# Token mixer of a two-layer diffusion backbone on one core: norms beside the products, gates and projections inside the attention steps

## The chip, the cores and the metric

The kernel runs on one core of a Trainium2 chip. Its time is the device time of one execution in microseconds (us). A core has TensorE (PE in the profile, its weight loads PEld), VectorE (DVE), ScalarE (ACT), GpSimd (POOL) and SyncE (SP, here the queue that loads weights). Each engine works through its own instructions in order and waits on semaphores that other engines raise.

## The reference, cut to what matters

Two layers over 640 tokens of width 1024: 512 latent tokens (tiles t = 0 to 3) and 128 context tokens (tile 4, called NS), in float32. The names on the left are those used below.

```python
mod = silu(cond) @ w_mod + b_mod                  # 6 x 1024 for each of 2 conditionings
sh1, sc1, g1, sh2, sc2, g2 = split(mod, 6)
h = rmsnorm(x, norm1_g) * (1 + sc1) + sh1
aq, ak, av, bu, bv, cq, ck, cv, gl = split(h @ w_in)     # 1792 columns (QKV), then 3 x 1024 (gates)
aq, ak, cq, ck = rmsnorm of each head of 64, then rotary angles
oa = windowed attention(aq, ak, av, cache_a, sink)       # branch A: 6 heads, blocks t-1, t, t+1, cache
ob = gelu(bu) * (w_s @ rmsnorm(gelu(bv)) + b_s)          # branch B
oc = full attention(cq, ck, cv, cache_c)                 # branch C: 6 heads, 4 blocks and cache
merged = sigmoid(gl[0])*(oa @ w_a_o) + sigmoid(gl[1])*(ob @ w_b_o) + sigmoid(gl[2])*(oc @ w_c_o)
x = x + g1 * (merged @ w_out)
h2 = rmsnorm(x, norm2_g) * (1 + sc2) + sh2
x = x + g2 * expert_choice_moe(h2)                       # 16 experts, 80 rows each, 96 weight chunks of 2 MB
```

## The kernel before

Both layers run the same program. Its stages follow each other on TensorE. Weights come in chunks of 8 x 128 rows by 512 columns (2 MB) into a ring of three slots, in one fixed order, issued by SP when a chunk's slot is free.

- **Conditioning, first part.** `mod_group` (line 617) multiplies `condT` (2 columns for each of 8 row blocks) by a 512-column chunk: 8 float32 products, each of which the trace shows as two instructions, 16 in all. Only 2 of the array's 128 columns are used. Four groups (MOD1) give shift and scale of the first norm; DVE adds the bias (L1205, L1209), 16 small transposes (L650) turn them into columns, and `h_out`/ACT L959 apply them to the transposed tiles (L605).
- **Products in three parts.** `group` (L628) multiplies one token tile by 256 columns: 24 instructions, high x high, high x low, low x high, in the rounded format. ACT makes the high part of the weights (WH, L947), DVE the low part (WL, L1183), both in two buffers of their own, so a ring slot is free as soon as it is split. QKV takes 7 x 5 = 35 groups; two PSUM banks of 256 columns are emptied in turn by ACT (L977) and DVE (L1233).
- **The rest of the conditioning and the norms.** Eight more `mod_group`s (MOD2), three of them right behind QKV, four between the turned heads and one inside attention; ACT copies the rows (L995), POOL adds biases (L494). After all of QKV, ACT does gelu and squares (L982, L989), DVE the sums (L1241), POOL the gains (L474), and DVE rotates queries and keys of both branches (L1254 to L1268, 5 tiles x 2 branches); TensorE turns them (L605).
- **Attention.** 60 units, one head of one tile each (`ORDER`). `scores` (L698, two heads side by side in the array's two row halves), masks (L706, float32), `reduce_max` (L1287) and the negative maximum (L1289, L1291) on DVE, exp on ACT (L1024), `turn` (L715), its copy out on DVE or ACT in turn (L1300, L1038), `weigh` (L726), and the scaled output (L1316). Nothing else but `mlp` (L686, branch B) and turned outputs lies among these steps.
- **Gates and projections.** 60 gate groups (L628, `split` again) and 60 projections (L775: float32, 2 or 3 row blocks of w_o by 256 columns, that is 4 or 6 instructions), ACT's tanh (L1061) and DVE's product (L1341, L1344), in the order A, B, C; group o+1 is issued ahead of projection o.
- **Output, router, experts.** 20 groups with w_out, second norm, router, top-k, then the experts (L857), with their own splits (L1090, L1440).

Of the kernel before, what the change touches and what calls it, by code (L numbers as in the profile page):

```python
# [5 lines left out]
D = 1024  # L20
# [8 lines left out]
MOD2_FIRST = 3  # L29
MOD2_AT = {2 * i + 1: MOD2_FIRST + i for i in range(MOD2 - MOD2_FIRST - 1)}  # L30
# [13 lines left out]
C_QKV = MOD1  # L44
C_MOD2 = C_QKV + (QU + 1) // 2
C_GATE = C_MOD2 + MOD2
C_WO = C_GATE + 9
C_MOE = C_WO + 2
CHUNKS = C_MOE + E * FFC
assert CHUNKS % RING == 0 and FFC % RING == 0 and C_MOE % RING == 0  # L50
LOADS = CHUNKS // RING
BRANCH = ((0, 1, 2), (6, 7), (3, 4, 5))


# [5 lines left out]
def unit_chunk(u):  # L60

    if u < U_GATE:
        return C_QKV + u // 2, u % 2
    if u < U_WO:
        b, q = divmod(u - U_GATE, 4)
        return C_GATE + 3 * b + 2 * (q // 2), q % 2
    return C_WO + (u - U_WO) // 2, (u - U_WO) % 2

G_QKV = MOD1
G_MOD2 = G_QKV + QU * NT
G_GATE = G_MOD2 + MOD2
G_WO = G_GATE + GU * NT
GROUPS = G_WO + WU * NT
GB = ((GROUPS + 1) // 2, GROUPS // 2)


def in_bank(g, b):

    return (g + 1 - b) // 2


def wo_group(w, t):

    return G_WO + (w * NT + t if w < 2 else 2 * NT + 2 * t + w - 2)


def last_group(u):

    if u < U_GATE:
        return G_QKV + u * NT + NT - 1
    if u < U_WO:
        return G_GATE + (u - U_GATE) * NT + NT - 1
    return wo_group(u - U_WO, NT - 1)

T_MOD, T_WS, T_CK, T_QK = 0, 1, 2, 3
T_MLP = T_QK + 2 * NT  # L100
T_O = T_MLP + NT
TQ = T_O + 2 * NT
# [4 lines left out]
UNITS = NT * 12  # L107
# [4 lines left out]
PAIR_ROWS = [6 * br + 3 * kv + g for br in range(2) for g in range(3) for kv in range(2)]  # L112
ORDER = [u for i in range(6) for u in [(i // 2, PAIR_ROWS[6 * (i % 2) + j]) for j in range(6)] +
         [(NS, PAIR_ROWS[2 * i + j]) for j in range(2)]] + [(NS - 1, r) for r in PAIR_ROWS]
LAST = [max(i for i, u in enumerate(ORDER) if u[0] == t) for t in range(NT)]

TURNS = {LAST[t] + 5 + 3 * h + 5 * (t == NS): (t, h) for t in (0, 1, 2, NS) for h in range(2)}
TURN_NO = {u: i for i, u in enumerate(list(TURNS.values()) + [(NS - 1, 0), (NS - 1, 1)])}
MLP_AT = {4 * t + 2: t for t in range(NT)}


def sinks_until(u):

    return sum(r < 6 for _, r in ORDER[:u + 1])


def unit(u):

    t, r = ORDER[u]
    br, h = divmod(r, 6)  # L130
    kv, g = divmod(h, 3)
# [6 lines left out]
    return t, br, kv, g, blocks  # L138


def build(nc, A, outs, scratch):
# [9 lines left out]
    with ctx:  # L151
# [7 lines left out]
        f32r = mybir.dt.float32r  # L159
        ring = sb("ring", [128, RING, KB, 512])  # L160
# [8 lines left out]
        qpair = EP[:, 512:1280].rearrange("p (b n) -> p b n", b=2)  # L169
        tmp = EP[:, 0:512]  # L170
        sqa, sqc, sqv = EP[:, 0:512], EP[:, 512:1024], EP[:, 1280:1536]
        hm = EP[:, 0:2 * D].rearrange("p (b n) -> p b n", b=2)
        gate_s = EP[:, 0:512].rearrange("p (b n) -> p b n", b=2)
        gated = EP[:, 512:768]
# [20 lines left out]
        condT = sb("condT", [128, 2 * KB])  # L195
# [13 lines left out]
        mx = sb("mx", [128, 4])  # L209
        nm = sb("nm", [128, 4])  # L210
        sm = sb("sm", [128, 4])
        es = sb("es", [128, 4])
        den = sb("den", [128, 1])
        rden = sb("rden", [128, 4])

        with ExitStack() as first:
            def sa(name, shape, dt=f32, scope=first):
                return scope.enter_context(nc.sbuf_tensor(name, shape, dt))

            with ExitStack() as rounded:  # L220
                HTH = sa("HTH", [128, NT, KB, 128], f32r, rounded)
            HT = sa("HT", [128, NT, KB, 128])
            with ExitStack() as split:
                WH = sa("WH", [128, 2, KB, 256], f32r, split)
                WL = sa("WL", [128, 2, KB, 256], f32r, split)
            MB = sa("MB", [128, 8 * D])
            Y = sa("Y", [128, NT * QKV])
            QK = sa("QK", [128, 8 * 640 + 2 * 768])
# [12 lines left out]

        modrow = Y[0:2, 0:2 * D]
        nrow1 = Y[0:2, 2 * D:3 * D]
        modrow2 = MB[0:2, 0:4 * D]
        bmod2 = MB[0:2, 4 * D:8 * D]
        nrow2 = bmod2[:, 0:D]
        gain2_part = bmod2[:, D:2 * D]
        y = Y[:, :].rearrange("p (t c) -> p t c", t=NT)
        merged = Y[:, 0:NT * D].rearrange("p (t d) -> p t d", t=NT)
        x1 = merged  # L250
        g1bc = Y[:, NT * D:(NT + 2) * D].rearrange("p (s d) -> p s d", s=2)
# [11 lines left out]

        ring_ready = [sem(f"ring_ready{s}") for s in range(RING)]
# [7 lines left out]
        par2_ready = sem("par2_ready")  # L272
# [6 lines left out]
        kv_saved = sem("kv_saved")  # L279
# [4 lines left out]
        cond_ready = sem("cond_ready")  # L284
        g_done = sem("g_done")
        g_free = [sem(f"g_free{b}") for b in range(2)]
        tq_done = sem("tq_done")
        tq_free = sem("tq_free")
# [5 lines left out]
        ROOTS = 2 * NT + 1  # L294
# [7 lines left out]
        gs_ready = sem("gs_ready")  # L302
# [8 lines left out]
        s_done = sem("s_done")  # L311
        nm_ready = sem("nm_ready")
# [6 lines left out]
        opj_done = sem("opj_done")  # L319
        opj_free = sem("opj_free")  # L320
# [32 lines left out]
        def chunk_src(l, c, e=None):  # L353

            if e is not None:
                w = (A["w_gate"], A["w_up"], A["w_gate"], A["w_up"], A["w_down"], A["w_down"])[c]
                n = (0, 0, 1, 1, 0, 1)[c]
                return w[l, e].rearrange("(k p) n -> p k n", p=128)[:, :, 512 * n:512 * n + 512]
            k0, k1 = 0, KB
            if c < C_QKV:  # L360
                w, lo, n = A["w_mod"], 512 * c, 512
            elif c < C_MOD2:
                w, lo = A["w_in"], 512 * (c - C_QKV)
                n = min(512, QKV - lo)
            elif c < C_GATE:
                w, lo, n = A["w_mod"], 512 * (c - C_MOD2 + MOD1), 512
            elif c < C_WO:
                br, i = divmod(c - C_GATE, 3)
                if i == 1:
                    w, lo, n, k0, k1 = A["w_o"], 0, D, BRANCH[br][0], BRANCH[br][-1] + 1  # L370
                else:
                    w, lo, n = A["w_in"], QKV + D * br + 256 * i, 512
            else:
                w, lo, n = A["w_out"], 512 * (c - C_WO), 512
            return w[l].rearrange("(k p) n -> p k n", p=128)[:, k0:k1, lo:lo + n]

        def slot_as(c, k, n):

            return ring[:, c % RING].rearrange("p k n -> p (k n)")[:, 0:k * n].rearrange("p (k n) -> p k n", k=k)
# [1153 lines left out]
```

## Time and profile before

| what | value |
|---|---|
| runs | 2824.15, 2825.93, 2835.42 us, median 2825.93 |
| profiled execution, its own time | 2830.99 us |
| its span, first to last instruction | 2829.2 us |
| mean granted TensorE clock | 0.929 of 2.4 GHz |
| instructions | 37290 |

The profile shows one execution. PE busy is a matmul's time from start to modelled end; consecutive matmuls overlap, so the distance between starts (the pitch) is what one costs. PEclk is the granted clock of TensorE as a share of 2.4 GHz; 0.5 is 1.2 GHz. "x" counts instructions. A run of n instructions on one row lasts (n - 1) pitches and one duration.

### The profile page before, as it was taken

To read this page: it belongs to the slowest core of one execution; us is meant where nothing else is said; L and a number is where in the kernel's file an instruction comes from. 1 tells how busy PE (TensorE), PEld (TensorE's weight loads), DVE (VectorE), ACT (ScalarE), POOL (GpSimd) and SP (SyncE) were. 2 spreads that over 40 slices of the span, in tenths; PEclk is the share of its full clock that TensorE was granted. 3 is DMA by queue.
4 is the path that set the end of the run, shared out by engine and by line. 5 is a ranking of instruction groups with operands and counts; after the bars stand their busy time and mean duration, and the time that the engine had idled before them with its cause. 6 is when DMAs were issued, how large, how long until landed. Compare 5 with 4: busy or idle time off the path is not lost.

```text
span 2829.2 us, 37290 instructions
## 1 busy us (share of the span) xinstructions
PE 2528.3 (89%) x14671; PEld 1915.1 (68%) x14671; DVE 1669.0 (59%) x2087; ACT 1195.6 (42%) x1414; POOL 378.3 (13%) x265
## 2 busy tenths in 40 slices
PE   5998899999949999999959989899999499999996
PEld 1964778989936666666529448799898266666664
DVE  2346542223567888889731664522345788888885
ACT  2222332112236666667531223411122366666664
POOL 1034000000021122211110430000000201221111
PEclk9998879999969999999979976999998699999998
DMA  8144000221539999999852530002224499999996
GB/s 299 46 169 156 1 1 16 75 82 38 224 111 333 359 372 373 368 370 377 309 204 75 175 120 1 1 16 75 83 100 165 165 336 358 373 370 374 374 375 224
DMA packets 267985, 568.76 MB, mean 201 GB/s; under 512 B 7056, under 2 KB 9280, under 8 KB 267760
## 3 DMA queue, kind: packets, MB, share of 16 engines
q1 hardware_dynamic: 251856, 512.25, 50.3%
q0 software_dynamic: 14416, 49.12, 5.9%
q10 hardware_dynamic: 1584, 5.57, 0.6%
q8 instruction: 92, 1.51, 0.2%
q14 instruction: 37, 0.30, 0.0%
HBM read 545.36 MB, written 26.80 MB: 202 GB/s over the span
## 4 chain that ended last, share of the span: by engine, by line
PE 47%; DMA 23%; DVE 16%; issue 7%; ACT 6%; DVEq 0%; ACTq 0%; SPq 0%; POOL 0%; POOLq 0%
PE ps L628 23%; DMA ring<-in_w_down 11%; DMA ring<-in_w_up 9%; PE ps L857 6%; DVE w_lo L1440 6%; PE ps L775 5%; ACT w_hi L1090 4%; PE ps L698 3%; PE ps L617 2%; PE ps L726 2%; PE ps L715 2%; PE ps L605 1%; DVE mx L1287 1%; PE ps L706 1%; DVE EP L1260 1%
## 5 line engine op out<-in xcount | busy, mean ns | idle before, releaser
L1440 DVE TENSOR_TENSOR w_lo<-ring,w_hi 128x2048 fp32r<-128x2048 f32 x378 | 859.0, 2285 | 165.1 <-ACT w_hi L1090 162.5
L1090 ACT ACTIVATE w_hi<-ring 128x2048 fp32r<-128x2048 f32 x384 | 722.0, 1916 | 350.0 <-DMA ring<-in_w_down 169.6
L857 PE MATMUL ps<-w_hi,xT 128*80 128x512 f32 x2048 | 647.9, 395 | 5.8 <-issue 3.5
L628 PE MATMUL ps<-WH,HTH 128*128 128x256 f32 x1840 | 541.9, 295 | 3.3 <-DVE WL L1183 3.3
L628 PE MATMUL ps<-WL,HTH 128*128 128x256 f32 x1840 | 520.6, 283 | 0.0
L628 PE MATMUL ps<-WH,HTL 128*128 128x256 f32 x1840 | 518.4, 282 | 0.0
L857 PEld LDWEIGHTS ps<-w_hi,xT 128*80 128x80 f32 x2048 | 305.4, 149 | 178.7 <-issue 9.2
L857 PE MATMUL ps<-w_lo,xT 128*80 128x512 f32 x1024 | 405.1, 396 | 0.0
L857 PE MATMUL ps<-w_hi,hT 128*80 128x512 f32 x1024 | 329.6, 397 | 29.9 <-DVE hT L1446 12.6
L628 PEld LDWEIGHTS ps<-WH,HTH 128*128 128x128 f32 x1840 | 349.7, 190 | 6.8 <-DVE WL L1183 3.7
L628 PEld LDWEIGHTS ps<-WH,HTL 128*128 128x128 f32 x1840 | 353.2, 192 | 0.0
L628 PEld LDWEIGHTS ps<-WL,HTH 128*128 128x128 f32 x1840 | 349.4, 190 | 3.1
L580 POOL DMA_INDIRECT x_save<-EP,idx x32 | 125.8, 3931 | 922.4 <-DVE EP L1455 922.4
L857 PEld LDWEIGHTS ps<-w_hi,hT 128*80 128x80 f32 x1024 | 152.8, 149 | 122.9 <-DVE w_lo L1440 15.8
L617 PE MATMUL ps<-ring,condT 128*2 128x512 f32 x384 | 174.4, 612 | 40.2 <-DMA ring<-in_w_mod 21.1
L857 PEld LDWEIGHTS ps<-w_lo,xT 128*80 128x80 f32 x1024 | 152.6, 149 | 79.5 <-issue 1.6
L1061 ACT ACTIVATE EP<-ps 128x256 f32<-128x256 f32 x120 | 45.9, 384 | 377.8 <-PE ps L628 377.8
L857 PE MATMUL ps<-w_lo,hT 128*80 128x512 f32 x512 | 202.6, 396 | 0.0
L1024 ACT ACTIVATE EP<-ps,nm 128x640 f32<-128x640 f32 (+3 forms) x120 | 77.4, 645 | 237.9 <-PE ps L715 83.7
L775 PE MATMUL ps<-ring,QK 128*128 128x256 f32 x640 | 163.1, 389 | 15.7 <-DMA ring<-in_w_o 14.4
L1344 DVE SCALAR_TENSOR_TENSOR EP<-EP,ps 128x256 f32<-128x256 f32 x80 | 33.6, 421 | 218.4 <-PE ps L775 218.4
L1287 DVE TENSOR_REDUCE mx<-ps 128x1 f32<-128x640 f32 (+3 forms) x120 | 75.9, 632 | 138.9 <-PE ps L698 138.9
(173 smaller groups left out, 2618.7 us busy)
## 6 DMA issues: line engine op xcount, KB each, us to landing
ring<-in_w_gate SPq DMA_DIRECT2D x64, 2048.0 KB, 9.4
ring<-in_w_up SPq DMA_DIRECT2D x64, 2048.0 KB, 9.5
ring<-in_w_down SPq DMA_DIRECT2D x64, 2048.0 KB, 11.5
ring<-in_w_mod SPq DMA_DIRECT2D x24, 2048.0 KB, 8.1
ring<-in_w_in SPq DMA_DIRECT2D x18, 2048.0 KB, 8.3
ring<-in_w_out SPq DMA_DIRECT2D x4, 2048.0 KB, 13.8
ring<-in_w_o SPq DMA_DIRECT2D x4, 1536.0 KB, 6.9
Y<-x_save POOLq DMA_DIRECT2D x10, 512.0 KB, 3.9
```

What stands on the lines that cost most here:

```text
L580: pool.indirect_dma_start(xs_d, bass.IndirectOffsetOnAxis(ap=idx[0:CE, e:e + 1], axis=0), eo[0:CE, e % 2], None, compute_op=ALU.add).then_ ...
L617: last = nc.tensor.matmul(ps[0:2, bank], condT.rearrange("p (s k) -> p k s", s=2)[:, k], ring[:, c % RING, k], start=k == 0, stop=k == KB - 1)
L628: last = nc.tensor.matmul(ps[:, g % 2, 0:256], a[:, t, k], w[:, u % 2, k], start=k == 0 and i == 0, stop=k == KB - 1 and i == 2)
L698: last = nc.tensor.matmul(ps[:, 2 * kv + i // 4, 128 * (i % 4):128 * (i % 4) + 128], qoT[r, 3 * br + g, 128 * t:128 * t + 128], kT[r, br, ...
L715: last = nc.tensor.transpose(ps[:, 4 + i // 4, 128 * (i % 4):128 * (i % 4) + 128], prob[:, u % 2, 128 * i:128 * i + 128], ident[:, :])
L726: last = nc.tensor.matmul(ps[:, 6, 0:64], probT[:, u % 2, 128 * i:128 * i + 128], v, start=i == 0, stop=i == len(blocks) - 1)
L775: last = nc.tensor.matmul(ps[:, 4 + o % 2, 0:256], qoT[:, k, 128 * t:128 * t + 128], w[:, i, 256 * q:256 * q + 256], start=i == 0, stop=k ...
L857: last = nc.tensor.matmul(ps[0:CE, bank], lhs[:, a, kb], w[:, u, k], start=kb == 0 and i == 0, stop=kb == KB - 1 and i == 2)
L1024: nc.scalar.activation(prob[:, i % 2, 0:n], ps[:, s0:s0 + 2].rearrange("p b n -> p (b n)")[:, 0:n], ACT.Exp, bias=nm[:, m], scale=SCALE, a ...
L1090: nc.scalar.activation(w_hi[:, u % UB], ring[:, raw[0], 4 * (u % 2):4 * (u % 2) + 4], ACT.Copy).then_inc(hi_ready, 1)
L1287: link(nc.vector.reduce_max(mx[:, m], ps[:, s0:s0 + 2].rearrange("p b n -> p (b n)")[:, 0:n], AX.X))
L1440: TT(w_lo[:, u % UB], ring[:, raw[0], 4 * (u % 2):4 * (u % 2) + 4], w_hi[:, u % UB].bitcast(f32), ALU.subtract).then_inc(lo_ready, 1)
```

## The change

The arithmetic is the same. What moves:

- `mod_group` puts the 8 row blocks into four column groups of the array (`tile_position=(0, 32 * q)`, `condT` widened to 32 columns), so that partial sums stand in four groups of PSUM partitions. They are added by a product with `fold` (for MOD1 merged with the transposes, for MOD2 `fold_rows`, one float32 product of 512 columns each). MOD2's eight groups and folds now stand inside the QKV loop (`MOD_AT`, `FOLD_AT`), through one ring slot.
- Ring chunks have hand-written slots (`PRE`); low parts overwrite the chunk (`ringL` lies on `ring`), so a slot is free only when its groups are done.
- QKV's PSUM is emptied 512 columns at a time from three banks. Squares, sums, rotation and turning of branch A and the gelu lie inside the QKV loop; branch C's norms come at the start of attention, its rotation and turning in steps 1 to 6.
- Attention goes in 30 steps, one for each pair of heads, A first and then C. Each step has three gaps (`FILL`) with gate groups, projections, branch B and turned outputs: 42 gates and 40 projections; 18 gates and 20 projections follow behind (`TAIL`). The order of branches is B, A, C. There is one PSUM bank for gates (6) and one for everything else (7). The mask product is in the rounded format.

```diff
+PRE = [(("mod", 0), 0), (("mod", 1), 1), (("mod", 2), 2), (("mod", 3), 0), (("qkv", 0), 1), (("qkv", 1), 2),
+       (("mod", 4), 0), (("mod", 5), 0), (("mod", 6), 0), (("qkv", 2), 1), (("mod", 7), 0), (("mod", 8), 0),
...
+SPLIT_AT = {-(-5 * u // 2): u + 1 for u in range(U_GATE - 1)}
+SPLIT_AT[15] = U_GATE
+MOD_AT = {3 + 4 * i: i for i in range(MOD2)}
+FOLD_AT = {5 + 4 * i: i for i in range(MOD2)}
+KA_AT = {25 + 2 * t: t for t in range(NT)}
...
+put(0, 0, "gate", 0)
+put(0, 0, "gate", 1)
+put(0, 0, "gate", 2)
+for n, (j, gap) in enumerate([(j, gap) for j in (1, 2, 3) for gap in (0, 2)] + [(j, 0) for j in range(4, 15)]):
+    put(j, gap, "gate", 3 + n)
+for t in range(NT):
+    put(2 + t, 0, "kc", t)
+    put(4 + t, 1, "mlp", t)
+    put(5 + t, 1, "mix", t)
+for n, (j, gap) in enumerate([(6, 2), (7, 2), (8, 2), (9, 2)] + [(j, gap) for j in range(10, 15) for gap in range(3)] +
+                             [(15, 0)]):
+    put(j, gap, "proj", n)
...
+LAGGED = lambda s: [x for o in range(20) for x in ([("gate", 20 * s + o)] + ([("proj", 20 * s + o - 1)] if o else []))] + \
+    [("proj", 20 * s + 19)]
+for n, (kind, i) in enumerate(LAGGED(1)):
+    put(15 + (n + 1) // 3, (n + 1) % 3, kind, i)
+TAIL = LAGGED(2)
...
@@ TensorE @@
+                        q = k % 4
+                        last = nc.tensor.matmul(ps[32 * q:32 * q + 32, bank], condT[:, k], ring[:, SLOT["mod", c], k],
+                                                start=k < 4, stop=k >= 4, tile_position=(0, 32 * q))
...
+                def fold_rows(i):
+                    pe.wait_ge(part_ready, l * MOD2 + i + 1)
+                    pe.wait_ge(mrow_ready, l * MOD2 + i)
+                    nc.tensor.matmul(ps[0:2, 5], fold[:, 0:2], modpart2, start=True, stop=True).then_inc(mrow_done, 1)
...
+                def gate(o):
+                    v, t = divmod(o, NT)
+                    if l or o:
+                        pe.wait_ge(gs_ready, l * GROUPS_G + o)
+                    group(ps[:, 6, 0:256], U_GATE + v, t).then_inc(gt_done, 1)
...
+                for j in range(NP + 1):
+                    if j < NP:
+                        scores(j)
+                    for kind, i in FILL[j][0]:
+                        extra(kind, i)
+                    if j:
+                        turn(2 * j - 2)
+                    for kind, i in FILL[j][1]:
+                        extra(kind, i)
+                    if j:
+                        turn(2 * j - 1)
+                    for kind, i in FILL[j][2]:
+                        extra(kind, i)
+                    if j:
+                        weigh(j - 1)
@@ ScalarE, QKV loop @@
+                    if p % 2 == 0:
+                        act.wait_ge(g_done, l * QG + min(2 * p + 2, QG))
+                        qkv_out(nc.scalar.copy, p).then_inc(g_free[p % 3], 1)
+                        if p:
+                            mod_part(p // 2 - 1)
...
+                split(U_GATE + 1)
+                evacuated(act, l, QP - 1)
...
+                nc.scalar.activation(sqa, y[:, :, CQ:CQ + 512], ACT.Square).then_inc(sq_ready, 1)
+                root(NT + 1, rs100[:, :, 8:20], st100[:, :, 8:20])
@@ ScalarE, attention @@
+                for j in range(NP + 1):
+                    for kind, i in FILL[j][0]:
+                        extra(kind, i)
+                    if j < NP:
+                        exps(j, 0)
+                    for kind, i in FILL[j][1]:
+                        extra(kind, i)
+                    if j:
+                        turned(j - 1)
+                    if j < NP:
+                        exps(j, 1)
+                    for kind, i in FILL[j][2]:
+                        extra(kind, i)
@@ VectorE @@
+                dve.wait_ge(s_done, l * NP + j + 1)
+                    link(nc.vector.tensor_reduce(mx[:, b], s_pair[:, :, 0:n], axis=AX.X, op=ALU.max))
...
+                split(U_GATE + 1)
+                sums(2, sqa, 8, 8)
+                mean_heads(8, 20)
+                dve.wait_ge(sd_ready, l * ROOTS + NT + 2)
+                nc.vector.reciprocal(rs100[:, :, 8:20], rs100[:, :, 8:20]).then_inc(rs_ready, 1)
...
+                    if j < NP:
+                        peak(j)
+                    for kind, i in FILL[j][0]:
+                        extra(kind, i)
+                    if j:
+                        turned(j - 1)
+                    if 1 <= j <= NT:
+                        rotate(1, j - 1)
...
```

## Rows read from the trace of the kernel before

**Rows 1.** The page, part 4: the chain that ended last, by line
```profile
PE ps L628 23%; DMA ring<-in_w_down 11%; DMA ring<-in_w_up 9%; PE ps L857 6%; DVE w_lo L1440 6%; PE ps L775 5%; ACT w_hi L1090 4%; PE ps L698 3%; PE ps L617 2%; PE ps L726 2%; PE ps L715 2%; PE ps L605 1%; DVE mx L1287 1%; PE ps L706 1%; DVE EP L1260 1%
```

**Rows 2.** Stages of layer 0: window, busy us (x) by engine, PEclk, DMA share, GB/s
```profile
0.00:78.20 78.20, 41.03 (x129) 15.23 (x130) 23.66 (x49) 26.22 (x46) 10.03 (x24) 0.91 0.77 271
78.20:178.60 100.40, 100.40 (x841) 100.27 (x841) 20.89 (x24) 16.19 (x23) 0.00 (x0) 0.98 0.21 74
178.60:242.50 63.90, 55.21 (x155) 13.62 (x154) 55.16 (x77) 23.34 (x52) 40.30 (x43) 0.98 0.63 223
242.50:442.90 200.40, 175.51 (x1217) 149.25 (x1217) 100.59 (x318) 67.94 (x188) 18.23 (x13) 0.79 0.07 23
442.90:704.30 261.40, 251.32 (x1826) 240.60 (x1825) 72.31 (x122) 49.29 (x83) 3.13 (x6) 0.98 0.15 53
704.30:829.70 125.40, 80.78 (x625) 79.32 (x626) 73.69 (x142) 25.95 (x34) 24.56 (x24) 0.77 0.44 161
829.70:1411.90 582.20, 561.95 (x2552) 361.70 (x2552) 487.19 (x314) 389.83 (x284) 91.58 (x29) 0.99 1.00 353
1411.90:1481.30 69.40, 40.30 (x126) 14.74 (x126) 23.89 (x49) 24.63 (x44) 8.88 (x14) 0.76 0.63 223
```

**Rows 3.** The chain in order of time, layer 0: start, us, what
```profile
27.43 29.58 PE ps L617 x64
...
78.19 100.48 PE ps L628 x840
...
472.86 1.29 PE ps L775 x6
474.15 2.83 PE ps L628 x24
```

**Rows 4.** The same, layer 1
```profile
1444.92 15.37 PE ps L617 x32
```

**Rows 5.** TensorE's groups by shape, both layers
```profile
L726 PE MATMUL ps<-Y,EP 128*128 128x64 f32 x672 | 105.7, 299 | 7.5 <-DVE Y L1316 7.0
L698 PE MATMUL ps<-QK 64*128 64x128 f32 x864 | 94.6, 356 | 28.4 <-ACT EP L1024 26.5 <-ACT QK L1009 1.5
L715 PE MATMUL ps<-ident,EP 128*128 128x128 f32 x432 | 86.6, 328 | 13.4 <-DVE EP L1300 7.2 <-ACT EP L1038 3.9 <-ACT EP L1024 2.1
L726 PE MATMUL ps<-cacheV,EP 128*128 128x64 f32 x192 | 42.4, 307 | 0.0
```

**Rows 6.** Timeline at full clock, heads with five blocks: start, us, instruction
```profile
1801.49 0.79 ACT L1024 ACTIVATE EP<-ps,nm 128x640 f32<-128x640 f32 x1 [1.17 <-DVE nm L1291]
...
1802.27 0.69 ACT L1038 ACTIVATE EP<-ps 128x640 f32<-128x640 f32 x1
...
1802.42 1.39 PE L698 MATMUL ps<-QK 64*128 64x128 f32 x20 [0.34 <-ACT EP L1024]
...
1803.84 0.82 DVE L1287 TENSOR_REDUCE mx<-ps 128x1 f32<-128x640 f32 x1 [1.36 <-PE ps L698]
...
1805.75 0.73 PE L715 MATMUL ps<-ident,EP 128*128 128x128 f32 x5 [0.18 <-DVE EP L1300]
...
1806.32 1.00 PE L726 MATMUL ps<-Y,EP 128*128 128x64 f32 x8
...
1807.16 0.39 PE L726 MATMUL ps<-cacheV,EP 128*128 128x64 f32 x2
```

**Rows 7.** ScalarE's groups, all of the run
```profile
L1061 ACT ACTIVATE EP<-ps 128x256 f32<-128x256 f32 x120 | 45.9, 384 | 377.8 <-PE ps L628 377.8
...
L995 ACT ACTIVATE MB<-ps 2x512 f32<-2x512 f32 x16 | 9.3, 584 | 73.1 <-PE ps L617 73.1
...
L926 ACT ACT_TABLE_LOAD x6 | 7.7, 1283 | 0.1
```

**Rows 8.** VectorE's groups by shape, 160 to 460 us
```profile
L1241 DVE TENSOR_REDUCE st<-EP 128x8 f32<-128x512 f32 x10 | 6.4, 681 | 6.3 <-ACT EP L989 6.3
```

**Rows 9.** The page, part 6: loads, KB, median us from issue to landing
```profile
ring<-in_w_mod SPq DMA_DIRECT2D x24, 2048.0 KB, 8.1
```

More of the change, by code:

```diff
@@ L28 @@
 MOD1, MOD2 = 4, 8
-MOD2_FIRST = 3
-MOD2_AT = {2 * i + 1: MOD2_FIRST + i for i in range(MOD2 - MOD2_FIRST - 1)}
+MODS = MOD1 + MOD2
 QU = QKV // 256
@@ L106, with pair @@
 HQ = 6 * NT
-UNITS = NT * 12
+NP = 2 * 3 * NT
+UNITS = 2 * NP
+GROUPS_G = GU * NT
 EPS = 1e-6
 SCALE = HD ** -0.5
[L112 to L131, printed above, removed]
+def pair(j):
+    n, g = divmod(j, 3)
+    br, t = divmod(n, NT)
     if t == NS:
@@ L381, in raw_of, with evacuated @@
+        def evacuated(engine, l, p):
+            for b in range(3):
+                n = len(range(b, p + 1, 3))
+                if n:
+                    engine.wait_ge(g_free[b], l * (QP // 3) + n + 1)
         def raw_of(j, b, first, s):
@@ new lines, in turn @@
+                def turn(v):
+                    n = len(pair(v // 2)[3])
+                    pe.wait_ge(e_ready, l * UNITS + v + 1)
+                    if l or v:
+                        pe.wait_ge(pt_evac, l * UNITS + v)
+                    for i in range(n):
+                        last = nc.tensor.transpose(psf[:, 1536 + 128 * i:1536 + 128 * i + 128],
+                                                   prob[:, v % 2, 128 * i:128 * i + 128], ident[:, :])
+                    last.then_inc(pt_done, 1)
@@ new lines, in weigh @@
+                def weigh(j):
+                    t, br, g, blocks = pair(j)
+                    pe.wait_ge(pt_evac, l * UNITS + 2 * j + 2)
+                    if l or j:
+                        pe.wait_ge(o_evac, l * NP + j)
+                    if j == 0:
+                        pe.wait_ge(mrow_ready, (l + 1) * MOD2)
+                    for kv in range(2):
+                        for i, b in enumerate(blocks):
+                            c = (AV, CV)[br] + 64 * kv
+                            v = cacheV[:, br, 64 * kv:64 * kv + 64] if b == NT else y[:, b, c:c + 64]
+                            last = nc.tensor.matmul(ps[:, 5, 64 * kv:64 * kv + 64], probT[:, kv, 128 * i:128 * i + 128], v,
+                                                    start=i == 0, stop=i == len(blocks) - 1)
+                    last.then_inc(pv_done, 1)
@@ new lines, in extra @@
+                def extra(kind, i):
+                    if kind == "gate":
+                        gate(i)
+                    elif kind == "proj":
+                        project(i)
+                    elif kind == "mlp":
+                        mlp(i)
+                    elif kind == "mix":
+                        mixed(i)
+                    elif kind == "out":
+                        outputs(i)
+                    else:
+                        turn_qk(1, i)
+                for j in range(NP + 1):
[13 more added lines that the diff above has]
+                        weigh(j - 1)
@@ L790, in _ @@
+                for kind, i in TAIL:
+                    extra(kind, i)
+                    if kind == "proj" and i > GROUPS_G - NT:
+                        merged_tile(i - GROUPS_G + NT - 1)
                 merged_tile(NT - 1)
```

1096 lines of the change are left out of this document (577 added, 519 removed).

## Prediction

> **What bounds the kernel now.** I read the chain of waits by line first: the three-part products (L628) lead it with 23% [rows 1], and behind them come weight loads of the experts. Then the stages of layer 0 [rows 2]. The experts move 353 GB/s with the DMA share at 1.00 for 582.2 us; the change doesn't touch them, and layer 1 repeats all stages. What is left is about 830 us a layer, and there three stages stand in a row that could overlap. In 178.6 to 242.5 us DVE is busy for 55.2 of 63.9 us with norms and rotation, and TensorE only has conditioning groups. In attention (200.4 us) all engines wait for each other in turn, and the granted clock averages 0.79 (of the two levels, 1.2 GHz for 42% of the time). The gates and projections (261.4 us) keep TensorE fully busy while DVE and ACT are idle for three quarters. So the question is how much real TensorE work attention holds.
>
> **Prices per instruction.** A group of 24 takes 2.83 us, a projection of 6 takes 1.29 us, which is 0.215 us for 256 columns in float32 [rows 3]; branch B's of 4 instructions take 0.86. With five blocks, turning a head costs 0.57 us (from its start to that of the weighing) and weighing it 10 x 0.105 = 1.05 us (8 of them in 0.84) [rows 6]. The 20 instructions of scores for two heads end in 1.39 us, at most 0.07 each. Alone, 128 columns would cost half of 0.215, that is 0.107, so the two row halves of the array do work side by side.
>
> **Conditioning in column groups.** 64 instructions of MOD1 last 29.58 us at 0.43 us or more each, one after another [rows 3], so a group of 16 costs 6.9 us. Column groups are not in this trace. The bounds are 0.107 us an instruction (all four overlap, 1.7 us a group) and 0.43 (none does, 6.9 us). Since the scores' halves overlap nearly in full, I take a factor of about 3, 2.2 us a group.
> The Trainium skill (TensorE: Matmul & The Clock Gate, "Measured speedup vs the span model" and "Why this matters for your kernels") has 3.07 times for four row tiles and 2.38 times for three column tiles; by 3.07 a group would cost 2.2 us and the time stay as forecast, by the lower bound of the row it would be some 8 us less, by the upper bound 100 more. The same skill (TensorEngine Tiling (Array Packing), "Key Properties") says that a change of tiling mode drains the array, which speaks against eight tiled groups amid QKV; no row here prices it.
> MOD1 in layer 0: the first chunk arrives at 27.4 us. The fourth can load only when the first group is done (32 us, at the low clock the engine starts with) and lands 8.1 us later [rows 9], so the groups end near 43.5 instead of 57.0 us. The fold inside the transposes adds 56 small instructions, some 4 us (at 0.07). QKV starts near 68.4 instead of 78.2 us: **-10**. In layer 1 DVE frees the banks only after the norm's first tiles, and the last two groups start at 1444.9 whatever they cost, and take 15.4 us [rows 4]; they would take 8 at the low clock, and the fold takes 5 back: **-2**.
>
> **QKV with MOD2 and the norms inside.** 35 groups: 99 us, as now (100.4). Eight conditioning groups 8 x 2.2 = 18, eight folds of two instructions of 512 columns, 8 x 0.86 = 7, five turned tiles 2.5 us. A wait is added: fold i stands right behind group 5 + 4i, and ACT makes its operand only after it has emptied the PSUM that this same group fills, two copies of 0.58 us [rows 7] and two handoffs. So TensorE, with all of QKV queued behind it, waits some 1.5 us eight times: 12 us. The sum is 138 against 100.4 + 63.9 = 164.3 us [rows 2]: **-26**. Squares, sums and the rotation of branch A are hidden beside 138 us of products, in which DVE has only 21 us of its own [rows 2] and gets about 45 more. The one load slot for conditioning chunks is covered too: 8.1 us to land [rows 9], one needed each 14 us. POOL's stores and reloads of bias rows have 28 us for each buffer.
>
> **Attention with the gaps filled.** Its own TensorE work: 432 scores at 0.065, 216 turns at 0.114, 432 weighings at 0.105 (half of the counts of both layers [rows 5]) make 28 + 25 + 45 = 98, masks, branch B and turned tiles about 15 (some 136 instructions at 0.11): 113 us. So of the 200.4 us over 85 are waits, though PE shows busy for 175.5. Filled in: 42 gates 119 us, 20 projections of B 17, 20 of A 26. Sum **275 us**. I add where the order makes TensorE wait all the same:
> - The start. ACT's split for gate 5 waits for all of QKV, then come squares of 2560 columns (2.2 us at ACT's rate of 640 columns in 0.79 less its start), DVE's split and sums (2.8 us, four to five times the 0.68 of 512 columns [rows 8]), and the root with a table load of 1.28 us [rows 7], then another for exp. Gates 0 to 2 share one bank, and gate 1 waits for the first tanh, which is queued behind all this on ACT. Step 0 takes about 19 us where its work is 10: +9.
> - Steps with four blocks or fewer. After scores (1.2) and a gate (2.8), ACT does tanh (0.38), exp, the copy of turned probabilities and exp again (0.7, 0.6, 0.9 with its row sum), so the pair is done near 8 us, and weighing waits about 1 us for the copy. 15 such steps: +12.
> - Steps 15 to 26, five blocks: scores 1.3, turns 1.1, weighing 2.1, and three items of the gaps 6.1 us, 10.6 us in all. Beside it DVE has its maximum of 1280 columns (2 x 0.82, less a start), and ACT 2 x 0.79 + 0.69 + 1.5 x 0.38 = 2.8 us and the reads of two row sums [rows 6, 7]: both are covered, and TensorE bounds the step. Handoffs 0.5 each: +6.
> - The last three steps have one block and few items: +8.
> Together **310 us**. Behind it the tail: 18 gates and 20 projections are 51 + 26 = 77, and 3 for the last tile: **80**. The stage now takes 200.4 + 261.4 = 461.8; 310 + 80 = 390: **-72**. I take the clock as full, since in the stages of dense products it stands at 0.98 [rows 2].
>
> **Edits costed at nothing.** Low parts in place hold each slot until its groups are done; a load (8 us) is covered by the five or more groups, 14 us, that still run from the other slot, and o_w for branch A and C by steps 15 and 29 to 30. If that cover went, each would cost up to its landing time of 8 us. Output stage, router and experts (125.4 + 582.2 us) keep their order; their first chunks load later, yet within these 125 us.
>
> **The sum.** Layer 0: 10 + 26 + 72 = 108; layer 1: 2 + 26 + 72 = 100; together 208 us. The span of 2829.2 becomes 2621; its own time lies 2 us above, the median of the runs 5 below that: **2618 us**.
>
> **Rivals.**
> - *Busy is busy.* If TensorE's 175.5 busy us in attention were work and not latency, the stage would be 175.5 + 251.3 = 427 and win 35 instead of 72 us a layer: 2618 + 74 = 2692. For it: the busy share of 88%. Against it: the pitches above. Chance 0.08.
> - *The order across engines bounds the steps.* Gates have one bank, so each waits for a tanh that ACT reaches only in its queue, behind exps that wait for DVE's maximum, which waits for DVE's part of a split. If each of 31 steps lost 2 us more: 2 x 62 us, 2742. For it: this kind of wait makes up attention today. Against it: the steps' margins of 2 to 5 us. Chance 0.14.
> - *Column groups don't overlap.* Then MOD2 costs 8 x 4.7 = 38 us a layer more and MOD1 gives nothing and takes its fold, 24 in both layers: 2618 + 100 = 2718. Chance 0.07. This is also the case in which the change doesn't do what it says.
> - *Slower: the low clock.* If the mixed steps kept TensorE at 1.2 GHz for all of attention, its 275 us of work a layer would take twice as long, since 1.2 GHz is half of the upper level: +550, 3170 us. It decides once about 105 extra us a layer are lost, that is with the low level for 38% of that work; today the stage is at 42%. Against it: the gates put dense products into every gap. Chance 0.04.
>
> **Numbers.** Forecast 0.65, busy 0.08, order 0.14, column groups 0.07, low clock 0.04, no change 0.02. In the forecast's own case the waits I added (2 x 35 + 2 x 12) may vanish, and full overlap gives 8 more: 2530 at the low end; the high end of this case is 2670. The range must take in busy and most of the column case: 2530 to 2720. Times within 0.5% of 2826 can't be told from no change. Faster 0.94, same 0.02, slower 0.04.
>
> **What would show it.** Right: the stage between QKV and attention is gone, QKV lasts near 138 us with eight short idle spots before the folds, waiting for ACT's copy; L617's counterpart has a pitch near 0.14 us; steps 15 to 26 last about 11 us each with PE's instructions end to end; PEclk near 1 in attention; the first gate's tanh waits some 7 us behind the root. Wrong: steps of 13 us or more with TensorE waiting for tanh or for copies; PEclk at 0.5 in long stretches; a pitch of 0.43 in the conditioning groups; TensorE waiting for chunks whose slot is held too long.

## The result, and the profile of the kernel after

The kernel after takes 2705.54 us in the median of 4 runs (2702.21 to 2706.07), beside 2829.61 us for the kernel before on the same chip: a ratio of 0.9559 (95% interval 0.9535 to 0.9583). It is faster by 124 us; the forecast was a gain of 208 us, that is 2618 us with a range of 2530 to 2720. The profiled execution's span went from 2829.2 to 2704.3 us.

The head of the page of the kernel after, and its chain by line, beside [rows 1]:

```profile
PE 2400.3 (89%) x14743; PEld 1875.3 (69%) x14743; DVE 1604.9 (59%) x1841; ACT 1187.4 (44%) x1350; POOL 352.1 (13%) x257
...
PEclk8899899999779999999959998999996899999998
...
PE ps L708 24%; DMA ring<-in_w_up 12%; DMA ring<-in_w_down 10%; PE ps L995 6%; DVE w_lo L1675 6%; PE ps L853 5%; ACT w_hi L1265 4%; PE ps L832 4%; PE ps L796 3%; PE ps L677 2%; PE ps L692 1%; DMA ring<-in_w_mod 1%; PE ps L816 1%; PE ps L931 1%; DVE EP L1690 1%
```

L708 is the old L628 (products in three parts), L692 the old L617 (conditioning groups), L853 the old L775 (projections), L832 and L796 weighing and scores. PEclk is not near 9 throughout: the digits 7 to 5 mark stretches at the lower of the two levels, 1.2 GHz, and some lie in stages that I had costed at 2.4 GHz.

The stages of layer 0 after, in the columns of [rows 2]; the last row is the conditioning stage of layer 1:

```profile
0.00:82.00 82.00, 39.13 (x184) 26.54 (x185) 24.05 (x54) 26.20 (x46) 12.04 (x28) 0.79 0.72 259
82.00:220.10 138.10, 128.34 (x1005) 107.04 (x1003) 46.14 (x59) 31.69 (x39) 14.79 (x25) 0.99 0.44 154
220.10:562.70 342.60, 313.94 (x2422) 286.85 (x2421) 142.72 (x303) 104.13 (x244) 16.23 (x25) 0.95 0.13 44
562.70:647.20 84.50, 82.33 (x598) 78.25 (x598) 29.16 (x52) 17.66 (x31) 2.87 (x4) 1.00 0.17 61
647.20:771.20 124.00, 79.60 (x618) 78.24 (x616) 73.26 (x141) 25.42 (x34) 25.74 (x23) 0.76 0.41 151
771.20:1349.10 577.90, 559.88 (x2556) 362.17 (x2559) 486.98 (x314) 389.42 (x284) 102.42 (x29) 0.99 1.00 356
1349.10:1420.90 71.80, 34.00 (x184) 25.19 (x184) 23.54 (x50) 24.59 (x44) 10.88 (x18) 0.61 0.60 213
```

| stage of layer 0 | before | forecast | after |
|---|---|---|---|
| until QKV starts | 78.2 | 68.4 | 82.0 |
| QKV, norms, conditioning | 164.3 | 138 | 138.1 |
| attention with its fill | 200.4 + 261.4 (gates behind it) | 310 | 342.6 |
| tail of gates and projections | in the above | 80 | 84.5 |
| w_out, router | 125.4 | 125.4 | 124.0 |
| sum, until the experts | 829.7 | 721.7 | 771.2 |

So layer 0 misses 49.5 us: 13.6 ahead of QKV, 0.1 in QKV, 32.6 in attention, 4.5 in the tail, less 1.4 behind it. Layer 1 shows the same: from QKV to w_out it takes 564.0 us against 627.4 before, and its conditioning stage is 2.4 us longer than before instead of 2 us shorter. The experts are as before (577.9 and 582.2 us).

**Ahead of QKV.** The chain of the kernel after in order of time:

```profile
28.05 3.67 PE ps L692 x16
...
31.74 12.43 DMA ring<-in_w_mod
...
44.21 3.41 PE ps L692 x16
...
48.97 0.31 PE ps L737 x2
...
63.27 0.51 PE ps L737 x2
63.78 0.87 PE ps L740 x8
```

The groups are short, but the chunks of weights land only at 28.1 to 44.2 us, so the groups end at 47.6 us instead of the forecast 43.5: the fourth chunk lands 12.43 us after the first group has freed its slot, where the prediction took 8.1 [rows 9]. Then the fold inside the transposes (L735 sums the four column groups while it turns them, L737 adds the bias) takes from 48.6 to 63.8 us, 15.2 us where the prediction had 4. From the end of the groups to QKV it takes 34.4 us, forecast were 24.9. The windows of the fold tell why: 0.155 us an instruction at first (0.31 for two), 0.26 later, and between them, at 50.4 us, the granted clock falls to its lower level.

```profile
48.60:50.90 2.30, 2.30 (x16) 2.19 (x15) 0.14 (x1) 1.28 (x1) 0.00 (x0) 0.95 1.05 387
50.90:63.80 12.90, 12.90 (x52) 12.51 (x53) 2.29 (x1) 2.43 (x2) 0.00 (x0) 0.50 0.66 243
```

**Attention.** The distances between the first scores of one step and of the next, taken from the timeline of L796 (us, step 0 first): 19.3, 11.7, 10.6, 11.4, **11.9, 12.5, 16.1, 14.7, 15.5**, 9.1, 11.2, 10.0, 9.0, 9.3, 8.1, 9.6; then twelve with the work of five blocks, mean 11.2; then 6.4 and the last one. Step 0 was forecast at 19 and the twelve at 11.1. What stands out are steps 4 to 8, 70.7 us. Of these the chain in order of time shows step 6 (its first scores start at 298.04 us):

```profile
302.22 5.04 PE ps L708 x24
307.26 0.45 PE ps L677 x4
...
307.73 0.45 ACT QK L1120
...
308.94 0.40 ACT QK L1202
...
309.48 1.09 PE ps L862 x8
...
310.79 0.67 DVE Y L1526 x3
...
311.60 1.10 PE ps L853 x4
312.70 1.73 PE ps L832 x16
```

L677 (turned keys and mixed tiles), L862 (branch B's mix) and L853 (a projection) all write the one bank 7. So TensorE writes it, ACT empties it (L1120, L1202), TensorE writes it again, DVE empties it (L1526), and only then come projection and weighing. TensorE waits 1.8 us (307.71 to 309.48; 0.67 us of it is an exp that stands between ACT's two copies in its queue) and then 1.0 us (310.57 to 311.60). And the gate group L708 in front takes 5.04 us where it takes 2.83 at 2.4 GHz: the granted clock is at 1.2 GHz from 296.2 to 306.4 us and again from 323.5 to 337.1.

These five steps do not take the same time in every trace. Where their order was not changed (the kernel after, e1, e2, e5 and e6, two layers each) they took 64.6 to 70.7 us, at a mean granted clock of 0.92 down to 0.83; layer 0 of the kernel after is at the long end, its layer 1 took 66.5.

### The profile page after: what moved, and what is told of

It is laid out like the page before. It is cut to its first block, busy times and chain, and to the rows that moved or that the text cites. A ratio compares the mean times of both kernels' runs of the same rounds, so it can differ in the third digit from the quotient of the medians.

```text
span 2704.3 us, 37126 instructions
## 1 busy us (share of the span) xinstructions
PE 2400.3 (89%) x14743; PEld 1875.3 (69%) x14743; DVE 1604.9 (59%) x1841; ACT 1187.4 (44%) x1350; POOL 352.1 (13%) x257
## 4 chain that ended last, share of the span: by engine, by line
PE 51%; DMA 25%; DVE 11%; ACT 7%; issue 6%; DVEq 0%; ACTq 0%; SPq 0%; POOL 0%; POOLq 0%
PE ps L708 24%; DMA ring<-in_w_up 12%; DMA ring<-in_w_down 10%; PE ps L995 6%; DVE w_lo L1675 6%; PE ps L853 5%; ACT w_hi L1265 4%; PE ps L832 4%; PE ps L796 3%; PE ps L677 2%; PE ps L692 1%; DMA ring<-in_w_mod 1%; PE ps L816 1%; PE ps L931 1%; DVE EP L1690 1%
## 5 line engine op out<-in xcount | busy, mean ns | idle before, releaser
L708 PE MATMUL ps<-WH,HTH 128*128 128x256 f32 x1840 | 543.5, 295 | 14.6 <-ACT Y L1190 9.1
L708 PE MATMUL ps<-ringL,HTH 128*128 128x256 f32 x1840 | 523.3, 284 | 0.0
L708 PE MATMUL ps<-WH,HTL 128*128 128x256 f32 x1840 | 522.5, 284 | 0.0
L708 PEld LDWEIGHTS ps<-WH,HTH 128*128 128x128 f32 x1840 | 355.0, 193 | 41.5 <-issue 23.4
L708 PEld LDWEIGHTS ps<-ringL,HTH 128*128 128x128 f32 x1840 | 355.4, 193 | 0.8
L708 PEld LDWEIGHTS ps<-WH,HTL 128*128 128x128 f32 x1840 | 354.3, 193 | 0.0
L853 PE MATMUL ps<-ring,QK 128*128 128x256 f32 x640 | 163.7, 389 | 16.0 <-ACT QK L1196 6.4
L1362 DVE TENSOR_TENSOR ringL<-ring,WH 128x2048 fp32r<-128x2048 f32 x46 | 105.4, 2290 | 82.4 <-ACT WH L1084 82.1
L853 PEld LDWEIGHTS ps<-ring,QK 128*128 128x128 f32 x640 | 112.7, 191 | 37.0 <-DVE Y L1537 9.9
L1084 ACT ACTIVATE WH<-ring 128x2048 fp32r<-128x2048 f32 x46 | 87.6, 1909 | 99.9 <-PE ps L708 69.3
L1190 ACT ACTIVATE SC<-ps 128x256 f32<-128x256 f32 x80 | 30.6, 383 | 221.0 <-PE ps L708 220.8
L1539 DVE SCALAR_TENSOR_TENSOR SC<-SC,ps 128x256 f32<-128x256 f32 x80 | 33.7, 421 | 155.9 <-PE ps L853 155.9
```

The lines of the kernel that those rows point to most:

```text
L708: last = nc.tensor.matmul(dst, a[:, t, k], w, start=k == 0 and i == 0, stop=k == KB - 1 and i == 2)
L853: last = nc.tensor.matmul(ps[:, 7, 0:256], qoT[:, k, 128 * t:128 * t + 128], w[:, i, 256 * q:256 * q + 256], start=i == 0, stop=k == ks[-1])
L1084: nc.scalar.activation(WH[:, u % 2], unit_cols(l, u, ring), ACT.Copy).then_inc(wa_hi, 1)
L1362: TT(unit_cols(l, u, ringL), unit_cols(l, u, ring), WH[:, u % 2].bitcast(f32), ALU.subtract).then_inc(wa_lo, 1)
L1539: STT(gated, gate_s[:, o % 2], 1.0, ps[:, 7, 0:256], ALU.add, ALU.mult).then_inc(side_free, 1)
```

## The experiments

Each but e7 is the kernel after with one edit; the diffs are shortened (`nc.tensor.` and some arguments are left out). Their runs stand beside runs of the kernel before on the same chip, at 2824.85 us (median) for e1 to e4 and 2828.1 for e5 to e7; ratios are to these, while the kernel after was timed beside 2829.61 us. So a difference in us to the kernel after crosses chips: of e1, e2, e3 and e5 it is -7, -18, -19 and -10 us, by their ratios it would be +2, -10, -14 and -5, and each of their intervals overlaps that of the kernel after. Only e4, e6 and e7 are clear of it. What the other four show is shown by their traces, since single runs of one kernel lie up to 16 us apart, those of the kernel before up to 42.

**e1: the fold in two loops.** First all 16 sums of the column groups, then all 16 bias products.

```
-for i, lo in enumerate((0, D)):
-    for k in range(KB):
-        n = 2 * (KB * i + k)
-        matmul(ps[:, 7, n:n + 2], modpart[:, lo + 128 * k:...], fold[:, 0:2], start=True, stop=False)
-        matmul(ps[:, 7, n:n + 2], modrow[:, lo + 128 * k:...], ident[0:2, 0:2], start=False, stop=True)
+for n in range(2 * KB):
+    matmul(ps[:, 7, 2 * n:2 * n + 2], modpart[:, 128 * n:...], fold[:, 0:2], start=n == 0, stop=False)
+for n in range(2 * KB):
+    matmul(ps[:, 7, 2 * n:2 * n + 2], modrow[:, 128 * n:...], ident[0:2, 0:2], start=False, stop=True)
```

> Edit: in the transposes behind MOD1, all 16 products with fold first, then all 16 products with the 2-row identity, instead of the two kinds in turn. In the changed kernel these 64 instructions and 8 transposes take 16 us in layer 0 (0.26 us each), where I had priced 0.07 each. Theory A: what costs is the alternation between products over 128 rows and over 2 rows; then they take 5 to 8 us in each layer and the kernel gets 16 to 22 us faster, about 2686. Rival B: what costs is the weight load of 128 x 128 float32 at the low clock, in any order; then 14 us or more stay and the kernel is within 5 us of 2705.

Measured: 2698.44 us (2691.16 to 2703.59), ratio 0.9566 (0.9502 to 0.9631). The chain of e1:

```profile
48.62 3.51 PE ps L733 x32
52.13 6.91 PE ps L736 x32
```

The fold takes 10.4 us instead of 15.2, and QKV starts at 77.3 instead of 82.0. In the first loop an instruction costs 0.11 us, in the second, which runs at 1.2 GHz, 0.216. So the two loops win 4.8 us in layer 0, and layer 1's stage ahead of QKV is 3.5 us shorter. Theory A expected 5 to 8 us for the fold, B 14 or more; 10.4 lies between them. An instruction costs 0.045 us less at either level of the clock, 2.9 us for all 64; the other 1.9 us come from the order too, since 32 instructions instead of 16 are through before the clock falls. The rest of my error is the low clock and the price of an instruction itself, which is no less than 0.11 here where I had taken 0.07. The timed difference of 7 us lies within what the intervals leave open; the place of the gain is shown by the trace.

**e2: each row fold one product group later.**

```
-FOLD_AT = {5 + 4 * i: i for i in range(MOD2)}
+FOLD_AT = {6 + 4 * i: i for i in range(MOD2)}
```

> Edit: each fold of MOD2 one product group later (behind group 6 + 4i instead of 5 + 4i), when ACT has made its operand. The trace of the changed kernel has 42 us of TensorE idle before the folds in both layers. Theory A: TensorE bounds QKV, so all of it comes back: 35 to 42 us, about 2665. Rival B: only half of it, 20 us, since the idle time is shared by both instructions' rows or by a wait for emptied banks that comes next: 2685. If DVE's rotations bound QKV, nothing: 2705.

Measured: 2687.59 us (2682.82 to 2696.52), ratio 0.9524 (0.9457 to 0.9591), 18 us under the kernel after. A fold of the kernel after, then one of e2, in the chain in order of time:

```profile
99.89 2.48 PE ps L708 x21
...
102.40 0.58 ACT Y L434
102.99 0.51 ACT SC L1113
...
103.58 1.02 PE ps L700 x2
```
```profile
99.94 5.41 PE ps L708 x46
105.35 0.95 PE ps L700 x2
```

After, TensorE waits from 102.38 to 103.58 us for ACT's two copies, 1.2 us; in e2 it goes from L708 into L700 without a pause. In the groups of the whole run:

```profile
L700 PE MATMUL ps<-SC,fold 128*2 128x512 f32 x32 | 16.3, 592 | 19.5 <-ACTq L1115 19.5
```
```profile
L700 PE MATMUL ps<-SC,fold 128*2 128x512 f32 x32 | 16.3, 592 | 0.0
```

The 19.5 us of idle time over 16 folds (first row: after) are gone in e2 (second row), and QKV is 9.3 us shorter in layer 0 and 8.8 in layer 1. The 42 us of idle time that my expectation set out from were misread: before these folds the trace has 19.5 us, both layers together. So nearly all of the wait came back, as theory A had it, but from half the amount. The wait that the prediction named was there, at 1.2 us instead of 1.5.

**e3: side products spread.** The mix of a tile turns in gap 0, branch B in gap 2, the gates of steps 4 to 8 in gap 1.

```
-... + [(j, 0) for j in range(4, 15)]):
+... + [(j, int(j < 9)) for j in range(4, 15)]):
     put(j, gap, "gate", 3 + n)
 for t in range(NT):
     put(2 + t, 0, "kc", t)
-    put(4 + t, 1, "mlp", t)
-    put(5 + t, 1, "mix", t)
+    put(5 + t, 0, "mix", t)
 ...
+for t in range(NT):
+    put(4 + t, 2, "mlp", t)
```

> Edit: in steps 4 to 8 of attention the gate moves from gap 0 to gap 1, branch B's turned tile to gap 0 and its mixing product to gap 2, so that no gap holds two small products in a row that need each other's PSUM bank. These five steps took 71 us in layer 0, forecast were 46, and the granted clock was at the low level in part of them. Theory A: the chain of small products with handoffs makes TensorE idle, and the idle time costs the clock; then the steps fall to about 50 us and the kernel gains 20 us a layer, 2665. Rival B: the steps are bound by DVE and ACT in their order (maximum, exp, copy, exp) whatever stands in the gaps: within 8 us of 2705, and the low clock stays.

Measured: 2686.06 us (2681.49 to 2693.51), ratio 0.9511 (0.9447 to 0.9575). Steps 4 to 8 take 10.6, 10.2, 11.9, 11.8 and 10.7 us, 55.2 in both layers in place of 70.7 and 66.5. The same 55 us of time in both, first after, then e3:

```profile
290.00:345.00 55.00, 48.95 (x306) 43.09 (x304) 19.02 (x51) 12.70 (x37) 2.23 (x4) 0.78 0.08 22
```
```profile
290.00:345.00 55.00, 50.18 (x410) 45.10 (x409) 24.97 (x63) 17.87 (x43) 2.23 (x4) 1.00 0.07 22
```

TensorE is about as busy in both, but works through 410 instructions instead of 306, since the clock stays at 2.4 GHz. Only the order changed, and theory A holds, if not in full (it expected 50 us). Against the spread of the unchanged order, 64.6 to 70.7 us, the gain is 9.4 to 15.5 us a layer; from the first scores to the experts e3 takes 10.9 and 10.7 us less than the kernel after in its two layers. The fall of the clock mostly goes with the waits on bank 7, but not always: in layer 1 of e7, in the same new order, it fell again from 1613.2 to 1620.1 us and the five steps took 58.2 us.

```profile
1575.00:1630.00 55.00, 51.17 (x402) 46.15 (x401) 25.80 (x68) 16.74 (x43) 2.22 (x4) 0.94 0.18 61
```

How the 15.5 us of layer 0 divide, e3 alone can't say. An estimate from the unchanged order: with 23.8 us at 1.2 GHz in these steps they took 70.7 us (after), with 10.2 us they took 64.6 (e5), so a microsecond at the low level costs about 0.45, the low clock makes up about 10.7 of the 15.5 us and the waits themselves about 5.

**e4: no fill.** All gates and projections of all branches go behind attention, in the order that the tail has; nothing is left out.

```
-put(0, 0, "gate", 0)
-put(0, 0, "gate", 1)
-put(0, 0, "gate", 2)
 for n, (j, gap) in enumerate(...):
-    put(j, gap, "gate", 3 + n)
+    pass
...
-    put(j, gap, "proj", n)
+    pass
...
-for n, (kind, i) in enumerate(LAGGED(1)):
-    put(15 + (n + 1) // 3, (n + 1) % 3, kind, i)
-TAIL = LAGGED(2)
-put(NP, 0, *TAIL.pop(0))
-put(NP, 1, *TAIL.pop(0))
+TAIL = LAGGED(0) + LAGGED(1) + LAGGED(2)
```

> Edit: no gates and no projections in the gaps of attention; all 60 of each follow behind it, in the same alternating order. Theory A (the forecast's): the gaps hide products in attention's waits, so this loses 35 to 45 us a layer: 2780 to 2795, with the low clock back in attention. Rival B: a step of two heads alone takes about 6.4 us by its chain (scores 1.4, maximum 1.7, two exps 2.0, copy 0.7, handoffs) where its TensorE work is 4.5, so the gaps hide little and what the change won lies in the conditioning, the norms and the pairing of heads: within 20 us of 2705.

Measured: 2972.78 us (2968.24 to 2976.14), ratio 1.0527 (1.0457 to 1.0598): 267 us slower than the kernel after and 148 slower than before. Both expectations fell short. Without the fill attention is only 49 us shorter (294 instead of 342.6), and the gates and projections behind it take 265 us instead of 84.5. Attention in e4, as a window and as the chain of a five-block step, beside it the same kind of step in the kernel after:

```profile
221.00:515.00 294.00, 234.15 (x1197) 199.20 (x1197) 99.04 (x227) 72.80 (x188) 17.48 (x25) 0.57 0.04 12
...
401.13 2.46 PE ps L789 x20
...
403.61 1.50 DVE mx L1479
...
405.22 0.83 DVE EP L1492
```
```profile
411.04 1.32 PE ps L796 x20
...
413.50 1.53 PE ps L853 x6
...
415.58 2.84 PE ps L708 x24
...
418.96 1.30 PE ps L853 x6
420.26 2.18 PE ps L832 x20
```

A five-block step holds a gate and two projections after, 5.7 us of work (2.84 + 1.53 + 1.30), and takes 11.2 us. Without this work it takes 11.1 us in e4 (mean of steps 16 to 26), because the 20 score instructions take 2.46 us instead of 1.32, DVE's maximum (L1479) and copy (L1492) stand bare on the chain, and the granted clock is 0.57 on average (0.50 in the step shown). So the fill in these steps costs nothing. Rival B's 6.4 us for such a step used prices of the full clock (scores 1.4 us). This is the low clock of my "slower" rival, met from the other side: it is what attention has without the fill, and the fill is worth 134 us a layer (267 / 2), where the expectation, which counted the hidden work alone, gave 45 at most. Why the clock here is lower still than before (0.79, [rows 2]) was not taken apart; the order of attention differs from the kernel before in several ways.

**e5: the split behind the first step.** The split of the sixth gate unit, ACT's copy and DVE's subtraction, is called in step 0 and no longer ahead of squares, sums and root.

```
-split(U_GATE + 1)
 evacuated(act, l, QP - 1)
 ...
+if j == 0:
+    split(U_GATE + 1)
 for kind, i in FILL[j][2]:
```

(and the same on VectorE, behind step 0's maximum.)

> Edit: the split of weight unit U_GATE+1 (a copy on ScalarE and a subtraction on VectorE of 128x2048 elements, 1.91 and 2.29 us in the trace) leaves its place ahead of the root and reciprocal between QKV and the first scores and goes behind the first step's peaks and exponentials. Theory A (engine order at the start costs what stands ahead in the queues): step 0 (19.3 us in the kernel after) or the way into it shortens by about 4 us per layer, 2705 to about 2697 us. Theory B (the third gate group of step 0 then waits for the split instead): within 4 us of the kernel after, the wait shows under the gate groups' line with ringL as its releaser.

Measured: 2695.66 us (2692.34 to 2708.62), ratio 0.9543 (0.9489 to 0.9597). Step 0 takes 17.1 us instead of 19.3. The chain of the kernel after at this place is as the prediction had it:

```profile
220.21 1.92 ACT WH L1084
...
222.15 2.29 DVE ringL L1362
224.44 2.79 DVE st L1446
...
227.75 1.28 ACT L1190
```

Of the 4.2 us of split (L1084, L1362) 2.2 are won at most: ACT's squares (2.35 us), which had lain beside DVE's half of the split, now stand on the chain themselves, so the sums (L1446) start at 223.45 instead of 224.44 us. Another 1.0 us is the first gate group, 4.53 instead of 5.50 us, since the clock is back at 2.4 GHz sooner. In direction theory A holds, in size it is half or less. The timed difference, 10 us, is more than 2 x 2.2; in this trace steps 7 and 8 are shorter too (12.2 and 11.9 us), with the clock at 1.00 in them. Nothing was changed there: it is the spread that e1 and e2 show in these steps as well, and why the clock comes back at different times is open.

**e6: no column groups.** The 16 conditioning instructions of a group go into one set of 32 output rows.

```
-q = k % 4
-last = matmul(ps[32 * q:32 * q + 32, bank], condT[:, k], ring[:, SLOT["mod", c], k],
-              start=k < 4, stop=k >= 4, tile_position=(0, 32 * q))
+last = matmul(ps[0:32, bank], condT[:, k], ring[:, SLOT["mod", c], k], start=k == 0, stop=k == KB - 1)
```

(copies and folds then take these 32 rows.)

> Edit: the conditioning products go one behind another into one set of 32 output rows instead of four column groups side by side; the sums over the four groups fall away with them. Theory A (column groups run at once): a group of 16 products goes from 1.92 us back to about 6.8 us at the full clock, 8 x 4.9 = 39 us more in QKV of each layer, and about 5 to 20 us more ahead of it, so about 2705 + 78 + 20 = 2800 us. Theory B (QKV has idle time in which the longer groups hide, or the groups wait for their chunk of weights anyway): at most 2740 us.

Measured: 2809.71 us (2805.09 to 2817.14, 10 runs), ratio 0.9935 (0.9902 to 0.9968): 104 us slower than the kernel after. L692's work in QKV of layer 0 after, and the same line in e6 (windows of that line alone):

```profile
82.00:220.10 138.10, 15.39 (x128) 3.33 (x128) 0.99 0.44 154
```
```profile
86.20:271.00 184.80, 56.43 (x128) 13.42 (x128) 0.96 0.33 115
```

A group of 16 takes 1.92 us after and 7.05 in e6, a factor of 3.7; my 2.2 us supposed about 3. QKV grows by 46.7 us in layer 0, of which 41.0 are these instructions, and by 41 in layer 1. Theory A, at 2800 us, holds: nothing hides them. Without the column groups about 20 of the change's 124 us are left, and my rival "column groups don't overlap", which priced their loss at 100 us, had the size right. The Trainium skill (TensorE: Matmul & The Clock Gate, "Measured speedup vs the span model") gives 3.07 for four row tiles and 2.38 for three column tiles; four column groups reach more here, and the measurement decides.
By the Trainium skill (TensorEngine Tiling (Array Packing), "Key Properties") a change of tiling mode drains TensorE. Here the step from L708 to L692 is 0.21 us from start to start instead of 0.12 within L708, and e6, without `tile_position`, and the kernel before (L628 to L617) show the same 0.21. So the tiled groups cost nothing extra at this place; whether the products of e6 and before count as the same mode for the chip, no run here shows.

**e7: e1, e2, e3 and e5 together.**

> Edit: the three edits that were faster alone (the fold in two separate loops, each row fold one product group later, the side products of the out tiles spread over other gaps) and the split behind the first step, together. Theory A (they stand in different stages, so they add): -7 -18 -19 and up to -8 us from 2705, about 2655 us, with QKV to w_out at about 540 us in layer 0. Theory B (what one frees another one's wait takes up, the weight chunks' landing first): 2675 us or more.

Measured: 2655.38 us (2646.78 to 2658.52, 6 runs), ratio 0.9384 (0.9344 to 0.9423). That beats both kernels: 50 us under the kernel after, and here the ratios say the same. The single differences were 7 + 18 + 19 + 10 = 54 us, but only about 26 by their ratios, so that theory A's 2655 us is met to the microsecond is luck. That the gains stand in different stages and add up is seen in the profile; its stages, to be read against those above:

```profile
0.00:78.20 78.20, 35.76 (x183) 23.11 (x184) 23.70 (x54) 26.19 (x46) 12.04 (x28) 0.78 0.76 271
78.20:207.50 129.30, 127.63 (x1006) 107.33 (x1005) 46.93 (x60) 31.57 (x39) 14.81 (x25) 0.99 0.48 165
207.50:530.00 322.50, 298.87 (x2419) 274.05 (x2418) 142.72 (x302) 104.62 (x244) 18.17 (x25) 0.99 0.14 47
```

Attention takes 322.5 instead of 342.6 us and QKV 129.3 instead of 138.1. Step 0 takes 15.5 us. In layer 1 QKV is 8 us shorter, and the stretch from the first scores to the experts another 8. QKV to w_out is 537.1 us in layer 0, against the 540 expected.

## Why the prediction was right in its range and 87 us off its number

- **The range: held, in part by luck.** The prediction set the high end of its own case at 2670 us and went up to 2720 only to take in the rivals "busy is busy" and "column groups don't overlap". 2705.54 us lies above 2670, and neither rival happened. (Its low end does not come out of its own terms either: 2618 less 94 of waits and 8 is 2516, not 2530; nothing hangs on it.)
- **What bounds and what overlaps: right.** The stage between QKV and attention is gone, gates and projections lie in attention, and the experts are unchanged. "Order across engines", "busy is busy", "column groups don't overlap" and "low clock for all of attention" did not happen as a whole.
- **QKV, forecast 138 us: measured 138.1.** Its terms hold too: 15.4 us for the eight groups (18), 8.2 for the folds (7), 1.2 us of wait each (1.5). These are 3.6 us less than forecast, so as much stands in no term, and the hit to 0.1 us is partly luck; layer 1's QKV is 2 us longer. e2 shows the waits by taking them away.
- **Column groups, forecast 2.2 us: 1.92** at the full clock. e6 shows that the change rests on them.
- **Step 0, forecast 19 us, and steps with five blocks, 11.1: measured 19.3 and 11.2.** The tail, forecast 80, took 84.5; its 4.5 us were not traced.
- **"MOD1 in layer 0 ... QKV starts near 68.4": failed, 13.6 us.** The term "56 small instructions, some 4 us (at 0.07)" was mis-sized: the fold took 15.2 us, and from the end of the groups to QKV it was 34.4 instead of 24.9, 9.5 us more. I took the pitch of the scores for them. Alternating between a sum over 128 rows and a bias product over 2 rows, an instruction takes 0.155 us at 2.4 GHz and 0.26 at 1.2; in loops of their own (e1) 0.11 and, at the low clock, 0.216. The other 4.1 us are the landing of the fourth chunk, priced at 8.1 us where it took 12.4. In layer 1 the same fold, forecast at 5 us, took 14.1 and made the −2 into +2.4, although the two groups there took 4.95 us instead of 8.
- **"Steps with four blocks or fewer ... +12": failed, about 30 us a layer.** Nearly all steps cost more than the sum, steps 4 to 8 by far the most. I had priced what the scores, probabilities and gates hand over, but not that turned keys, mixed tiles, branch B's mix, outputs and projections share bank 7 and that several fall into one step. That is a chain of TensorE, ACT, TensorE, DVE, TensorE ahead of the weighing. It is my "order across engines" rival in five steps of 31. e3 shows 9 to 15.5 of the 30 us by moving only these; the rest is spread over the other steps and wasn't traced to a cause.
- **"I take the clock as full": failed in parts.** In 290 to 345 us it is 0.78, in the fold 0.50. In e3 the same stretch has 1.00 without any work removed, so the order decides most of it. e4 shows what it is without fill, 0.57.

The 87 us between the medians are 83 between the spans (2704.3 and 2621), 49.5 of them in layer 0. e7 wins 50 us with four small changes of order. What remains lies in the landing of the first conditioning chunks, in the fold, and in attention's other steps, where nothing was tried.

## What to carry to other kernels

Fill the gaps of a latency-bound stage with dense products even where the stage gets no shorter by it: here the fill was free in the five-block steps, and with it the granted clock was 0.95 instead of 0.57. When several small products share one accumulator bank, spread them over different gaps, since each hand-over by another engine stands bare on TensorE's path; and put a product that needs another engine's copy one group behind the earliest place. A first estimate for tiny products should be taken from rows of the same shape or from an upper bound: here the products of the fold cost 0.11 us at least, not 0.07.

## What the runs showed of the hardware that was not expected

Four column groups of 32 columns overlap almost fully in float32: 16 instructions of 512 columns in 1.92 us, against 7.05 in one column group. The granted clock fell to 1.2 GHz while TensorE was busy without a pause by the profile, in the fold: busy from 44.2 us on, the fall at 50.4, then 12.90 of 12.90 us busy with 52 small instructions, at 0.50. A fold that sums over 32 rows instead of 128 (e6) took 0.11 us an instruction at 2.4 GHz even in alternation, against 0.155 with 128 rows. So neither the alternation alone (e6) nor the 128 rows alone (e1, 0.11) has the higher price, only both together. In e6 too the clock fell to the lower level on the way:

```profile
63.17 0.22 PE ps L736 x2
63.39 0.42 PE ps L734 x2
```
